# RWKV-7 and S5 hybrid layer: six changes of order and of the norms' factors

## The reference

```python
def hybrid_layer(x, shift0, wkv0, s5r0, s5i0, p):
    x = x + 0.5 * swiglu(rmsnorm(x, p['g_ffn1']), p['ffn1_gate'], p['ffn1_up'], p['ffn1_down'])
    h = rmsnorm(x, p['g_mix'])
    proj = h @ p['w_in']
    ...
    y_a, wkv = rwkv7_branch(f_mix, wkv0, p)
    y_b, s5r, s5i = s5_branch(u, s5r0, s5i0, p)
    merged = gates[..., :D_MODEL] * (y_a @ p['w_a_up']) + gates[..., D_MODEL:] * (y_b @ p['w_b_up'])
    x = x + (merged @ p['w_out']).astype(x.dtype)
    ...
```

## Time and profile before

| what | value |
|---|---|
| time, median of 3 runs | 2463.25 us (2461.17 to 2464.54) |
| profiled execution: its own time | 2463.62 us |
| its span | 2461.8 us |
| TensorE busy | 2415.3 us (98%) |
| VectorE busy | 1282.6 us (52%) |
| GpSimd busy | 1057.5 us (43%) |
| ScalarE busy | 579.2 us (24%) |
| mean granted TensorE clock | 0.993 |

### The profile page before, as it was taken

One profiled execution on the slowest core, in us unless ns is written; L12 is line 12 of the kernel. 1 busy time (PEld: TensorE's weight loads), 2 busy tenths in 40 slices (PEclk: granted clock), 3 DMA queues, 4 the chain that ended last, 5 costly groups with the idle time before them and its releaser, 6 DMA issues. The chain is left out here.

```text
span 2461.8 us, 50035 instructions
## 1 busy us (share of the span) xinstructions
PE 2415.3 (98%) x21418; PEld 2363.9 (96%) x21418; DVE 1282.6 (52%) x1843; ACT 579.2 (24%) x1084; POOL 1057.5 (43%) x604
## 2 busy tenths in 40 slices
PE   8999999999999999999998999999999999999998
PEld 8999999999999999999997888899999999999998
DVE  5851871671336255552466766566754444453225
ACT  4000010010011000011336676412433333341001
POOL 3434444334444344422340000254686868775550
PEclk9999999999999899999999999999999999999999
DMA  3111211211114432633451100072121212153211
GB/s 141 43 53 50 75 62 51 69 52 59 52 37 177 100 95 86 177 87 105 147 189 59 33 18 19 30 252 92 69 100 64 94 62 92 63 186 106 75 52 69
DMA packets 93733, 211.94 MB, mean 86 GB/s; under 512 B 16464, under 2 KB 42704, under 8 KB 92816
## 3 DMA queue, kind: packets, MB, share of 16 engines
q1 hardware_dynamic: 67184, 157.96, 19.7%
q10 hardware_dynamic: 26400, 51.82, 6.6%
HBM read 154.39 MB, written 54.20 MB: 85 GB/s over the span
## 5 line engine op out<-in xcount | busy, mean ns | idle before, releaser
L179 POOL TENSOR_TENSOR whi<-wraw,small 128x1024 fp32r<-128x1024 f32 (+3 forms) x136 | 232.5, 1710 | 846.0 <-PE ps L213 772.3
L213 PE MATMUL ps<-hhi,whi 128*128 128x344 f32 x1848 | 396.5, 323 | 0.0
L213 PE MATMUL ps<-hlo,whi 128*128 128x344 f32 x1848 | 393.2, 321 | 0.0
L213 PE MATMUL ps<-hhi,wlo 128*128 128x344 f32 x1848 | 391.3, 320 | 0.0
L182 POOL TENSOR_TENSOR wlo<-wraw,whi 128x1024 fp32r<-128x1024 f32 (+3 forms) x136 | 332.2, 2443 | 10.7
L213 PEld LDWEIGHTS ps<-hlo,whi 128*128 128x128 f32 x1848 | 313.8, 190 | 0.0
L213 PEld LDWEIGHTS ps<-hhi,whi 128*128 128x128 f32 x1848 | 310.9, 189 | 1.9 <-issue 0.7
L213 PEld LDWEIGHTS ps<-hhi,wlo 128*128 128x128 f32 x1848 | 309.2, 189 | 0.0
L3476 PE MATMUL ps<-t_hi,whi 128*128 128x258 f32 x704 | 143.8, 286 | 3.0 <-ACT ffn_gate L3383 1.0
L3476 PE MATMUL ps<-t_lo,whi 128*128 128x258 f32 x704 | 142.2, 283 | 0.0
L534 ACT ACTIVATE tmp<-tmp 128x1032 f32<-128x1032 f32 x22 | 23.5, 1068 | 504.2 <-DVE tmp L455 487.8
(11 more groups left out here) (511 smaller groups left out, 5052.2 us busy)
## 6 DMA issues: line engine op xcount, KB each, us to landing
wraw<-ffn_up SPq DMA_DIRECT2D x44, 512.0 KB, 3.3
wraw<-ffn_down SPq DMA_DIRECT2D x40, 384.0 KB, 3.1
wraw<-ffn_up SPq DMA_DIRECT2D x11, 1024.0 KB, 4.9
weights_raw_b<-ffn_up SPq DMA_DIRECT2D x11, 1024.0 KB, 4.8
a_spilled<-ffn_gate SPq DMA_DIRECT2D x18, 516.0 KB, 2.7
a_raw<-a_spilled SPq DMA_DIRECT2D x18, 516.0 KB, 4.0
wraw<-w_mix SPq DMA_DIRECT2D x18, 512.0 KB, 3.4
gates<-gate_out ACTq DMA_DIRECT2D x16, 516.0 KB, 2.9
```

Of the source, the lines that this page charges most:

```text
L179: pool.tensor_tensor(g.whi[:, s, 0:n], g.wraw[:, s, 0:n], g.zero.to_broadcast([P, n]), ALU.add).then_inc(g.w_hi, 1)
L213: last = pe.matmul(g.ps[:, 3 * bank_set + b, 0:BLK], w[:, s, k * P:(k + 1) * P], x(k, b), start=(k == 0 and first), stop=(k == kt - 1 and ...
```

## The change

1. **The norms' factors as rounded parts.** A new function `small_parts` makes from the table of factors a high part, rounded to fp32r, and the rest as a low part (two more VectorE operations ahead of `rstd_small`). `rstd_pe` now does two products for a group of tokens, with an identity in fp32r that VectorE copies once at the start. This holds for the norms of `rstd_pe`; the last norm keeps its fp32 products.
2. **RWKV keys.** In VectorE's turn `decayed(p)` comes behind `level(q, 5)` in place of ahead of it.
3. **A wait.** Before the turns TensorE waits for set 0 alone; the wait for set 1 stands ahead of the first scores, which are the first to write there.
4. **Output's first units.** Of the first two units of `w_out`, TensorE does tiles 0 to 5 of both, then tiles 6 and 7 of both.
5. **Last thirds.** The three pieces of tokens of the last stage are 430, 344 and 258 columns in place of 344 each, through new functions `third`, `third_len` and `third_sums`.
6. **First x tile.** Columns 0 to 343 of tile 0 come by ACT's queue, the others by SP's queue behind weight unit 0. The counts that wait for tile 0 are 16 higher. One table (`seg`) is loaded with 72 columns in place of 128.

```diff
--- before.py
+++ after.py
             pe.wait_ge(g.rstd_ready, 3 * n + 1)
-        last = pe.matmul(g.ps[:, 6 + (j // 5) % 2, (j % 5) * SS:(j % 5 + 1) * SS],
-                         g.small[0:SS, 1, j:j + 1].to_broadcast([SS, P]), g.ident[0:SS, 0:SS],
-                         start=True, stop=True)
+        for part in range(2):
+            last = pe.matmul(g.ps[:, 6 + (j // 5) % 2, (j % 5) * SS:(j % 5 + 1) * SS],
+                             g.small_r[0:SS, part, j:j + 1].to_broadcast([SS, P]), g.ident_r[0:SS, 0:SS],
+                             start=part == 0, stop=part == 1)
         if j in (4, 9, 11):
...
     rsqrt(v, st, y, x, t, 1.0 / D, NORM_EPS)
+    small_parts(v, g, st, y)
     v.sem_inc(g.rstd_small, 1)
...
+
+def small_parts(v, g, st, y):
+
+    hi, lo = (g.small_r[0:SS, part, 0:NSS] for part in range(2))
+    st.do(v.tensor_copy(hi, y))
+    st.do(v.tensor_tensor(lo, y, hi.bitcast(F32), ALU.subtract))
 
...
+            v.wait_ge(g.c_in, 16 * 2)
+            st.do(v.tensor_copy(g.ident_r[:, :], g.ident[:, 0:SS]))
...
             newton()
+            small_parts(v, g, st, y)
             v.sem_inc(g.rstd_small, 1)
...
             if p is not None and not last:
                 key_norm(p)
-                decayed(p)
             if q is not None:
                 level(q, 5)
...
                 sample_t(3)
             if p is not None and not last:
+                decayed(p)
                 inverse_decayed(p)
                 bonus(p)
...
+    g.set1_free = use[1] + (GATES + WT + DT) // 2 + 1
...
                     next(rest)
-            for j in range(2):
-                pe.wait_ge(g.set_free[j], use[j] + (GATES + WT + DT) // 2 + 1)
+            pe.wait_ge(g.set_free[0], use[0] + (GATES + WT + DT) // 2 + 1)
             for _ in rest:
...
+            if c == 0 and p == 0:
+                pe.wait_ge(g.set_free[1], g.set1_free)
...
-            with pe.Fori(0, DT // 2 - 1) as i:
+            for h, ks in enumerate((range(DT - 2), range(DT - 2, DT))):
...
-                    product(pe, g, i, 2, uo + j, DT, j, use_o[j], 1, part(g.mhi), part(g.mlo),
-                            (g.m_split, lambda i, k: k + 1))
+                    if h == 0:
+                        pe.wait_ge(g.w_split, uo + j + 1 + WSLOTS)
+                        pe.wait_ge(g.set_free[j], use_o[j] + 1)
+                    for k in ks:
+                        pe.wait_ge(g.m_split, k + 1)
+                        for w, x, first in ((g.whi, g.mhi, True), (g.whi, g.mlo, False), (g.wlo, g.mhi, False)):
+                            for b in range(NBLK):
+                                last = pe.matmul(g.ps[:, 3 * j + b, 0:BLK], w[:, (uo + j) % 2, k * P:(k + 1) * P],
+                                                 part(x)(k, b), start=k == 0 and first,
+                                                 stop=k == DT - 1 and w is g.wlo)
+                    if h:
+                        last.then_inc(g.unit_done, 1)
+            with pe.Fori(0, DT // 2 - 2) as i:
+                for j in range(2):
+                    product(pe, g, i, 2, uo + 2 + j, DT, j, use_o[j] + 1, 1, part(g.mhi), part(g.mlo))
...
-TPB = BLK // SS
+LAST_TOK = (0, 430, 774, TOK)
...
-def last_acc(g, u):
-    return g.ps[:, 5 - 5 * (u % 2), 0:BLK]
+def third(c):
+    return slice(LAST_TOK[c], LAST_TOK[c + 1])
...
+def third_len(c):
+    return LAST_TOK[c + 1] - LAST_TOK[c]
...
+def third_sums(c):
+    return slice(LAST_TOK[c] // SS, LAST_TOK[c + 1] // SS)
...
+def last_acc(g, u, c):
+    return g.ps[:, 5 - 5 * (u % 2), 0:third_len(c)]
...
-                        last = pe.matmul(last_acc(g, u), w[:, n * P:(n + 1) * P], x[:, c * BLK:(c + 1) * BLK],
+                        last = pe.matmul(last_acc(g, u, c), w[:, n * P:(n + 1) * P], x[:, third(c)],
...
-                v.scalar_tensor_tensor(x, last_acc(g, u), 0.5, x, ALU.mult, ALU.add).then_inc(g.set_free[u % 2], 1)
+                v.scalar_tensor_tensor(x, last_acc(g, u, c), 0.5, x, ALU.mult, ALU.add).then_inc(g.set_free[u % 2], 1)
...
-        for j in range(TPB * c, TPB * (c + 1)):
+        for j in range(third_sums(c).start, third_sums(c).stop):
...
-        for j in range(TPB):
+        for j in range(third_len(c) // SS):
...
-                             g.small[0:SS, 1, TPB * c + j:TPB * c + j + 1].to_broadcast([SS, P]), g.ident[0:SS, 0:SS],
+                             g.small[0:SS, 1, LAST_TOK[c] // SS + j:LAST_TOK[c] // SS + j + 1].to_broadcast([SS, P]), g.ident[0:SS, 0:SS],
...
+        sp.dma_start(g.x[:, 0, BLK:TOK], a["x"][:, 0, BLK:TOK]).then_inc(g.x_in[0], 16)
...
-        sp.dma_start(g.seg[:, :], a["tabs"][:, T_SEG, :]).then_inc(g.c_in, 16)
+        sp.dma_start(g.seg[:, :], a["tabs"][:, T_SEG, 0:SEG_COLS]).then_inc(g.c_in, 16)
...
-        for k in range(0, DT, 2):
+        act.dma_start(g.x[:, 0, 0:BLK], a["x"][:, 0, 0:BLK]).then_inc(g.x_in[0], 16)
+        for k in range(2, DT, 2):
...
-                act.wait_ge(g.x_in[k], 16)
+                act.wait_ge(g.x_in[k], 16 if k else 32)
...
-        v.wait_ge(g.x_in[n], 32)
+        v.wait_ge(g.x_in[n], 32 if n else 48)
```

More of the change, by code:

```diff
@@ L34 @@
 NSS = TOK // SS
+SEG_COLS = 72
 L8 = 8
@@ L117, in plan @@
     g.ident, o = at("ident", o, [P, P])
-    g.seg, o = at("seg", o, [P, P])
+    g.seg, o = at("seg", o, [P, SEG_COLS])
     g.small, o = at("small", o, [P, 6, 16])
     g.zero = g.small[:, 5, 0:1]
+    g.small_r = at("small_parts", o - (3 * 16 * 4 + 31) // 32 * 32, [P, 2, 16], F32R)[0]
     g.rstd, o = at("rstd", o, [P, TOK])
     g.s5p, o = at("s5_persistent", o, [P, 4, J])
+    g.ident_r, o = at("ident_rounded", o, [P, SS], F32R)
     g.hhi, o = at("hhi", o, [P, DT, TOK], F32R)
@@ L3326, in _ @@
             if u < DT:
-                v.wait_ge(g.x_in[k], 48)
+                v.wait_ge(g.x_in[k], 48 if k else 64)
             elif b:
@@ L3625, in build @@
     n1 = g.norms + 1
-    def third(c):
-        return slice(c * BLK, (c + 1) * BLK)
     def final_act(act):
@@ L3637, in final_act @@
                     act.wait_ge(g.ssum_step, DT * n1 + q - 1)
-                act.activation(g.tmp2[:, q % 2, 0:BLK], g.xd[:, k, third(c)], ACT.Square).then_inc(g.sq_ready, 1)
+                act.activation(g.tmp2[:, q % 2, 0:third_len(c)], g.xd[:, k, third(c)], ACT.Square).then_inc(g.sq_ready, 1)
                 if c and k == DT - 1:
@@ L3651, in add_square @@
             v.wait_ge(g.sq_ready, DT * n1 + q + 1)
-            total, sq = g.ssum2[:, third(c)], g.tmp2[:, q % 2, 0:BLK]
+            total, sq = g.ssum2[:, third(c)], g.tmp2[:, q % 2, 0:third_len(c)]
             if k == 0:
@@ L3660, in factors @@
             v.wait_ge(g.norm_ss, n1 + 1 + c)
-            x, y, t = (g.small[0:SS, a, TPB * c:TPB * (c + 1)] for a in range(3))
-            st.do(v.tensor_copy(x, g.ps[0:SS, 6, TPB * c:TPB * (c + 1)]))
+            x, y, t = (g.small[0:SS, a, third_sums(c)] for a in range(3))
+            st.do(v.tensor_copy(x, g.ps[0:SS, 6, third_sums(c)]))
             rsqrt(v, st, y, x, t, 1.0 / D, NORM_EPS)
@@ L3669, in scale @@
             x = g.xd[:, k, third(c)]
-            v.scalar_tensor_tensor(x, x, g.vec[:, V_GF + k:V_GF + k + 1], g.ps[:, 2 + c, 0:BLK], ALU.mult, ALU.mult)\
+            v.scalar_tensor_tensor(x, x, g.vec[:, V_GF + k:V_GF + k + 1], g.ps[:, 2 + c, 0:third_len(c)], ALU.mult, ALU.mult)\
              .then_inc(g.y_ready, 1)
```

## The result

The changed kernel takes 2474.59 us (2471.17 to 2475.53, 6 runs) against 2462.97; the ratio is 1.0046, with a 95% interval from 1.0036 to 1.0056. It is 11.6 us slower where 1.9 had been forecast (2465.2), and outside the range. One single execution of all kernels stood apart, 3904.98 us at a granted clock of 0.555 with the split keys and the thirds; no ratio contains it.

The account below looks back on a forecast made before the run. TensorE was taken as the bound, busy 2415.3 of 2461.8 us. Terms 0 + 2.3 + 0 + 2.35 - 1.25 - 1.5 = +1.9 took the median from 2463.25 to 2465.2 us; range 2458.5 to 2469.0.

Parts of the forecast that it names:

- Taken: 0: Three norms' factors: the value chosen for rounded parts, with the two extra vector operations taken as hidden, +0.3 if not.
- A: Norms' factors as rounded parts: 24 products and weight loads a norm as before, so 0; about -2.8 if loads were hidden.
- The smaller seg load and the copy of ident lie far from the chain: 0: Table load and identity copy that come with the rounded factors: no effect on the time, 0.
- B: RWKV keys, decayed(p) behind level(q, 5): level wait won, VectorE then late for the scores, +2.3 us, from -4.1 to +3.0.
- +0.34: RWKV turn: rw_bv starts 0.34 us later, so TensorE's second pair of score products does too; counted in six turns.
- C: Wait for accumulator set 1 before the turns: it only changes its name to rw_eye, 0; bound -1.2 us.
- D: Output's first two units: TensorE waits for GpSimd's split of unit 2, +2.35 us, from 0 to +3.5; the 1.07 wait stays.
- The rival of the slower side: Clock falls in the new wait at output's unit 2: +3.6 us on top, +5.5 in all, 2468.8; chance 0.13.
- E: Last thirds of 430, 344 and 258 columns: shorter tail against a longer middle, -1.25 us, from -0.8 to -1.8.
- about +0.35 with loads: Last stage's first third: two more factors and two more sums in the middle of TensorE's work, about +0.35 us.
- F: First x tile over two queues: TensorE starts some 1.85 us earlier, at 7.2; -1.5 us kept, from -0.5 to -1.9.
- not all is kept: First unit: the last tiles are bound by total bytes, so of some 1.85 us earlier start 1.5 remains.

Follow-up runs that it names:

- the split keys and the thirds: Kernel before with only the last of decayed's three operations behind level 5, plus last pieces of 430, 344 and 258 columns: 2457.76 us, ratio 0.9982.
- parts unused: A alone, but factors spread with the earlier fp32 products; VectorE makes rounded parts and identity that nothing reads: 2466.12 us, ratio 1.0015.
- the layout alone: Kernel before with only the rounded factors' memory layout (seg of 72 columns, 352-byte gap, later tiles 128 bytes up), fp32 factors: 2463.80 us, ratio 1.0007.
- A alone: Kernel before with only the norms' factors as rounded parts, with fp32r identity, shorter seg and moved addresses: 2467.56 us, ratio 1.0023.
- E's kernel: Also E alone: kernel before with only the last pieces of 430, 344 and 258 columns: 2461.54 us, ratio 0.9993.
- all but F: Changed kernel with the first x tile loaded as before: 2473.60 us, ratio 1.0045.
- D alone: Kernel before with only the order of output's first two units changed: 2465.33 us, ratio 1.0012.
- the changed kernel with 60 waits: Changed kernel plus 60 VectorE waits, for a count long reached, ahead of the first norm's factors: 2472.69 us, ratio 1.0045.
- B alone: Kernel before with only decayed(p) moved behind level(q, 5): 2465.16 us, ratio 1.0009.
- F alone: Kernel before with only the first x tile split over two queues: 2463.55 us, ratio 1.0003.

## Why the prediction was wrong

**The step that failed is "Taken: 0" for A**, together with "The smaller seg load and the copy of ident lie far from the chain: 0". The products were read rightly: 24 records, 2.77 against 2.81, loads of 192 ns against 190, and VectorE's operations were hidden where they stand. What the sum left out is that seven operations lengthen VectorE's program and that 128 bytes move all tiles behind. The first costs 3.4 us near 1260 against the profile before, or 3.0 over the 0.4 that the profiles without it lose there on average, far from the edit. That the operations carry it, parts unused against the layout alone shows; that they do so by the place of a code load rests on the 20 profiles above. A part is the longer wait (2.12 in A alone, 0.72 in E's kernel, at the same product) and a part a fall of the clock to the 1.2 GHz level (granted 0.79 for 8 us, so 1.7 us); the second costs 0.9 us. Together 3.9 of the 5.7 measured; the other 1.8 is inside the interval. In the three profiles of the changed kernel and of all but F, 1.6 us more is lost at the third norm in a fall of the clock right behind the factors. Such a fall behind the second or the third norm's factors is in four of the eight profiles with rounded products and in none of the twelve others, so A may bring it now and then; why, and why not always, was not settled.

**B was right in mechanism and too small.** VectorE was late for `rw_bv` and the loss came back at the scores. The term "+0.34" a turn measured 0.52 in the timeline; the period of `rw_bv` went from 35.8 us ((1465.5 - 1358.1) / 3) to 36.4 ((1471.5 - 1362.3) / 3). I carried durations over and left out that decayed begins 0.22 behind the operation that it follows, which the earlier trace rows show ahead of it in the kernel before. Over six turns the start of `rw_bv` moved by 3.3 us in B alone and 3.7 in the changed kernel, for +2.3; the time of B alone, +2.2 with an interval from 0 to +4.4, can't tell them apart.

**C** was right: 0, the wait changed its name.

**D** was right: +2.35 was forecast, +2.3 came in the changed kernel. The wait of 1.07 did not stay; it is 0 to 0.9 in the other profiles, with D and without. The rival of the slower side, a fall of the clock in this wait, is real: D alone and the changed kernel with 60 waits show it, at +1.6, not +3.6.

**E**, -1.25: the tail won 1.4 (the sums' first product is at +11.9 against before, the end at +10.5), the middle lost 1.0 in place of 0.35. The term mis-sized is "about +0.35 with loads": TensorE waits 0.5 for the sums of squares in the middle, so VectorE was not covered there. E alone's profile has the tail at 1.0 in place of 1.4, because its last sums ran at the 1.2 GHz level, and nothing won in all; its time, -1.7 with 2.2 to each side, leaves all of this open.

**F**, -1.5: the start came 2.0 earlier (7.02 for 9.04), but F alone against E's execution of the old start (7.21 for 8.65) won 1.4, and 0.4 is left behind the first unit; the mean of all profiles is 1.6 and 0.8. The step "not all is kept" was right, its size and its reason wrong. The prediction named the last tiles. In F alone the lead is gone by 13.5 us, at the slow pace of the first products. In the first profile of the changed kernel, where that pace ends at 10.0, TensorE waits 0.94 for VectorE's last low part at 21.0.

Sum of what the traces show in the changed kernel, against the sum of +1.9: A +3.9 and +1.6 at the third norm, B +3.7, C 0, D +2.3, E -0.4, F -0.8: +10.3, measured +11.6 (8.9 to 13.8). Of the miss of 9.4, A is 5.5.

## What to carry to other kernels

An edit that adds instructions or bytes moves everything behind it: look for the cost in stages that it does not touch, by following the same instruction through both traces. In an order written out by hand, move the smallest piece that fills the wait: one third of `decayed` gave 3.0 to 3.5 us where all of it cost 2 to 3. A wait that an edit adds to TensorE can be followed by a stretch at the lower clock: 1.6 us on top of D's 2.3, in two of six profiles.

## What the runs showed of the hardware

- A load of 8 KB of program during a 256 KB weight load went with 1.6 us more for the latter on average (7.4 to 7.8 from issue to use, against 5.4 to 6.9), in six of six profiles.
- An fp32r weight load of 86 x 128 took 188 to 192 ns, as the fp32 one (188 to 193): fp32r factors gain nothing over fp32 ones here, since the product with two rounded parts has as many records as the fp32 product.
- Moving the tiles by 128 bytes made the second FFN's products 0.2% slower (0.9 us in 445, eight profiles); by 256 bytes it did not (two profiles).
- Stretches at the 1.2 GHz level followed waits of TensorE of 2.0 to 2.5 us in some executions and not in others: D's wait of 2.04 had one behind it in two profiles of six, the wait of 2.04 to 2.48 near 1260 in six of six. Each lasted 3.4 us and cost 1.6 to 1.7.
- In the first microseconds three fp32r products of 344 columns took 1.06 us, and 0.63 from 10 to 15 us on, in all profiles; an earlier start was in part spent at the slow pace.
